# Fetching an expert block's output rows whole instead of in two halves

## The reference

```python
g_sel = jnp.argmax(g_logits, axis=-1)                       # one of 4 groups
top_p, top_i = lax.top_k(jax.nn.softmax(e_logits), 2)       # 2 of its 8 experts
# every (token, expert) pair gets a row; rows are sorted by expert, and each
# expert's rows are padded to blocks of 128
hid = jax.nn.silu(xb @ w_gate[e]) * (xb @ w_up[e])          # per block of 128 rows
y_rows = hid @ w_down[e]
y = zeros.at[row_token].add(y_rows * row_weight)            # two rows end on each token
```

## Time and profile before

| | |
|---|---|
| median of 3 runs | 1632.38 us (1631.96 to 1632.64) |
| profiled execution | 1631.91 us, its span 1630.2 us |
| busy, share of the span | PE 96%, DVE 78%, ACT 44%, POOL 37% |
| weights' queue (issued by SyncE), packets' time | 46.7% of the 16 DMA engines' span |
| GpSimd's queue, packets' time | 4.3% |
| output rows: fetches, scatters | 64 and 64 transfers |

### The profile page before, as it was taken

One profiled execution on the slowest core, in us unless ns is written; L12 is line 12 of the kernel. 1 busy time (PEld: TensorE's weight loads), 2 busy tenths in 40 slices (PEclk: granted clock), 3 DMA queues, 4 the chain that ended last, 5 costly groups with the idle time before them and its releaser, 6 DMA issues. The chain is left out here.

```text
span 1630.2 us, 26227 instructions
## 1 busy us (share of the span) xinstructions
PE 1572.4 (96%) x7516; PEld 1273.8 (78%) x7516; DVE 1268.1 (78%) x2301; ACT 716.7 (44%) x1219; POOL 601.5 (37%) x746
## 2 busy tenths in 40 slices
PE   6999999999999999999999998999999999999996
PEld 5778888878888788888888887777777777777774
DVE  6668868868778678688687786988878888888884
ACT  5333232223332323332322442765566666666662
POOL 2222131131130221321311311375666666655554
PEclk9999999999999999999999986999999999999999
DMA  4121121221121221211212665999999999999992
GB/s 158 39 83 54 50 78 34 59 73 46 41 74 42 60 72 45 65 50 49 79 33 72 198 229 187 352 361 369 365 375 370 378 369 372 356 367 364 375 362 81
DMA packets 142996, 292.76 MB, mean 180 GB/s; under 512 B 21596, under 2 KB 72204, under 8 KB 142896
## 3 DMA queue, kind: packets, MB, share of 16 engines
q1 hardware_dynamic: 127904, 266.29, 46.7%
q0 software_dynamic: 14992, 25.22, 4.3%
HBM read 291.81 MB, written 25.30 MB: 195 GB/s over the span
## 5 line engine op out<-in xcount | busy, mean ns | idle before, releaser
L2038 DVE TENSOR_TENSOR gu_lo<-w_gu,gu_hi 128x1024 fp32r<-128x1024 f32 x256 | 307.0, 1223 | 55.2 <-ACT gu_hi L1878 40.2
L1305 PE MATMUL proj<-uTh,wl 128*128 128x512 f32 x768 | 308.7, 402 | 7.4 <-issue 4.6
L1307 PE MATMUL proj<-uTh,wh 128*128 128x512 f32 x768 | 301.1, 392 | 0.0
L1306 PE MATMUL proj<-uTl,wh 128*128 128x512 f32 x768 | 300.0, 391 | 0.0
L1878 ACT ACTIVATE gu_hi<-w_gu 128x1024 fp32r<-128x1024 f32 x256 | 264.0, 1055 | 81.0 <-PE g_ps L1951 37.0
L556 POOL TENSOR_TENSOR wl<-raw,wh 128x512 fp32r<-128x512 f32 x96 | 129.5, 1366 | 382.3 <-ACT wh L643 382.3
L1305 PEld LDWEIGHTS proj<-uTh,wl 128*128 128x128 f32 x768 | 144.9, 189 | 37.9 <-issue 7.5
L1307 PEld LDWEIGHTS proj<-uTh,wh 128*128 128x128 f32 x768 | 144.7, 188 | 31.7
L696 ACT ACTIVATE xbc<-v 128x512 f32<-128x512 f32 x64 | 40.5, 633 | 292.1 <-DVE v L1021 292.1
L1306 PEld LDWEIGHTS proj<-uTl,wh 128*128 128x128 f32 x768 | 145.2, 189 | 28.6
L1021 DVE SCALAR_TENSOR_TENSOR v<-xr,cw,v 128x512 f32<-128x512 f32 x192 | 146.1, 761 | 14.7 <-DVE v L1017 0.5
(11 more groups left out here) (301 smaller groups left out, 3295.0 us busy)
## 6 DMA issues: line engine op xcount, KB each, us to landing
w_gu<-in_moe_w_gate_dram SPq DMA_DIRECT2D x128, 512.0 KB
w_gu<-in_moe_w_up_dram SPq DMA_DIRECT2D x128, 512.0 KB
w_d<-in_moe_w_down_dram SPq DMA_DIRECT2D x128, 512.0 KB
raw<-in_ssd_w_in_dram SPq DMA_DIRECT2D x96, 256.0 KB, 3.3
E<-acum_dram SPq DMA_DIRECT2D x64, 256.0 KB, 3.5
raw<-in_ssd_w_out_dram SPq DMA_DIRECT2D x28, 256.0 KB, 2.9
hacc<-in_x_dram SPq DMA_DIRECT2D x8, 512.0 KB, 7.5
out_dram<-hacc SPq DMA_DIRECT2D x8, 512.0 KB, 5.6
```

Source lines behind the costliest of these rows:

```text
L1305: nc.tensor.matmul(out, al, bh, start=start, stop=False)
L1306: nc.tensor.matmul(out, ah, bl, start=False, stop=False)
L1307: return nc.tensor.matmul(out, ah, bh, start=False, stop=stop)
L2038: vec.tensor_tensor(wl[:, j % RING, :], weights.gate_up(b, j), wh[:, j % RING, :].bitcast(F32), ALU.subtract).then_inc(w_lo, 1)
```

## The change

A fetch becomes one indirect transfer of 1024 columns per row, from `out` itself, with the token numbers in `stmp` as indices. Before it is issued it waits for both halves of the scatter. There is one semaphore per buffer instead of two, and `y_out` waits for it once, before the first half's add. Scatters stay in halves.

```diff
-        fetched = [[sem(f"fetched{b}{h}") for h in range(2)] for b in range(2)]
+        fetched = [sem(f"fetched{b}") for b in range(2)]
...
-                wait(pool, held_done, p, b, 4, -behind)
+                wait(pool, held_done, p, b, 3, -behind)
...
-            def fetch(p, b, h):
-
-                if b == 1:
-                    wait(pool, scattered[0][h], p, 0, 8, 16)
-                else:
-                    wait(pool, scattered[1][h], p, 0, 8, 0)
-                g.tensor_tensor(held[:, 1 + h, :], zero[:], zero[:], ALU.add).then_inc(held_done, 1)
-                g.indirect_dma_start(yb[:, b, h * 512:(h + 1) * 512], None, half_rows,
-                                     bass.IndirectOffsetOnAxis(sidx[:, b, h:h + 1].bitcast(U32), 0),
-                                     bounds_check=last_half, oob_is_err=False).then_inc(fetched[b][h], 16)
+            def fetch(p, b):
+
+                for h in range(2):
+                    if b == 1:
+                        wait(pool, scattered[0][h], p, 0, 8, 16)
+                    else:
+                        wait(pool, scattered[1][h], p, 0, 8, 0)
+                g.tensor_tensor(held[:, 1, :], zero[:], zero[:], ALU.add).then_inc(held_done, 1)
+                g.indirect_dma_start(yb[:, b, :], None, out,
+                                     bass.IndirectOffsetOnAxis(stmp[:, b, 0:1].bitcast(U32), 0),
+                                     bounds_check=last_token, oob_is_err=False).then_inc(fetched[b], 16)
...
-                    for h in range(2):
-                        fetch(p, b, h)
+                    fetch(p, b)
...
                 for j in range(2):
-                    wait(dve, fetched[b][j], p, 0, 8, 16)
+                    if j == 0:
+                        wait(dve, fetched[b], p, 0, 8, 16)
                     wait(dve, y_mm, p, b, 2, j + 1)
```

More of the change, by code:

```diff
@@ L1854, in _ @@
             last = pairs(pool, table_first)
-            wait(pool, held_done, last, 1, 4, 2)
+            wait(pool, held_done, last, 1, 3, 1)
             for h in range(2):
```

## The result

| | before | after |
|---|---|---|
| median of 4 runs each, us | 1632.51 | 1656.22 |
| lowest to highest | 1631.96 to 1635.44 | 1651.20 to 1671.47 |
| profiled execution, us | 1631.91 | 1657.26 |
| its span, us | 1630.2 | 1654.1 |

A forecast was written before the change was run, and what follows sets the result against it. The prediction took TensorE as the bound in the middle and latency at the end; 3.4 (end) + 1.2 (first blocks) + 0 (middle) = +4.6 us gave 1636.5 profiled, 1637.0 us as median, range 1634.0 to 1645.0.

The forecast's parts named there:

- The end: Last two blocks, nothing covering them: two whole fetches of 4.2 us each count fully, +3.4 us (+1.6 to +5.4).
- The first blocks: First expert blocks: whole fetches land later and TensorE waits for the adds, +1.2 us (-0.9 to +2.5).
- The middle: Expert blocks under streaming weights: the whole fetch lands before the next add is due, cost 0, 0.9 us left.
- The place: Middle: the whole fetch issues in the second half's place, 1294.34, leaving 8.5 us to the add at 1302.86.
- The landing: Middle, weights streaming: a whole fetch lands 7.6 us after its issue, bounds 6.4 and 8.8.
- the middle stalls: Rival, chance 0.18: with a landing of 8.8 the middle's loop outlasts 18.47 us, 0.3 per block, +7.5, 1644.5 us.
- The estimate from the page: Every whole fetch: the second half's 0.13 MB at 436 GB/s adds 0.3 us, sum about 1635; not used in forecast.
- The rival that went by 0.3: Rival, chance 0.20: second half costs 0.3 us, end +2.2, first blocks about +0.5, 1635.1 us, within the noise.

The follow-up runs named there:

- e12: Kernel before, half fetches each behind its own scatter, but the first add waits for both halves' fetches; 1635.69 us, ratio 1.0016.
- e13: Kernel before, but the first half's fetch waits for both halves of the scatter, adds wait for their own half; 1652.24 us, ratio 1.0102.
- e9: Changed kernel, but the last pair of blocks fetches in halves with a wait for each, as before; 1657.10 us, ratio 1.0138.
- e1: Changed kernel run once more, unchanged, against the kernel before on the same chip; 1661.16 us, ratio 1.0181.
- e4: Changed kernel with the gather of input rows issued ahead of the fetch instead of behind it; 1647.69 us, ratio 1.0096.
- e2: Kernel before, fetches in halves, but the first fetch waits for both scatters and the first add for both fetches; 1691.05 us, ratio 1.0345.
- e7: Kernel before with half of the weights' bytes loaded from block 2 on; 1629.97 us, ratio 0.9961.
- e3: Changed kernel, but its one fetch brings only the first 512 columns, the second half unread; 1632.58 us, ratio 1.0001.
- e14: Changed kernel fetching only one half of the columns, with the gather issued ahead of the fetch; 1634.63 us, one execution.
- e8: Changed kernel with half of the weights' bytes loaded from block 2 on; 1630.93 us, ratio 0.9967 to the kernel before.
- e11: Changed kernel, but VectorE begins a block's splits only once GpSimd has issued the fetch; 1655.69 us, ratio 1.0151.
- e10: Kernel before, halves everywhere, with the gather issued ahead of the two fetches; 1638.88 us, ratio 1.0039.
- e5: Changed kernel, with VectorE computing three unused tiles, both operands in SBUF, before its last adds; 1661.79 us, one execution.
- e6: Changed kernel, with VectorE computing four unused tiles, one operand in PSUM, before its last adds; 1657.50 us, one execution.

## Why the prediction was wrong

**The end: right up to the last scatter's issue, with nothing put behind it.** Forecast +3.4, measured +3.1. A whole fetch with quiet engines takes 4.33 and 4.36 us (4.2 forecast), 1.05 over the half's 3.30. The 0.53 us of issue ahead of the last fetch were not in the sum; the fetch of block 30 went out 0.7 us earlier after block 29's adds than before (1625.14 to 1631.73, against 1601.53 to 1608.82). These two errors cancel in part. e12 shows that the join at the adds alone makes this price (23.9), e13 that the join at the fetch alone makes 1.9 of it (22.7), and e9 takes it away.

Behind that issue the sum had no term, as if the rest stayed as it was. It is 2.9 us shorter to the end of the span. So of the +3.1 only +0.3 is left there (28.7 and 29.0; 29.1 in e1, 29.9 in e4), and the price of the end is far below the forecast. The cause is open.

**The first blocks: one landing too small.** The first whole fetch is added 20.6 us after block 0's adds, 20.9 forecast. The second is issued 31.2 us after them (31.3 forecast), in GpSimd's timeline after:

```profile
1073.73 2.03 POOL L1804 DMA_INDIRECT yb<-out_dram,stmp  x1
...
1092.76 1.70 POOL L1804 DMA_INDIRECT yb<-out_dram,stmp  x1 [0.52 <-issue]
```

but it is added 10.5 us later (1103.24), where I had 8.8. The first four blocks lose 3.9 us in place of 1.2.

**The middle: the step that failed.** It brings 15.6 of the 19.5 us from block 0 to 29. It read: "The whole fetch has the second half's place: issue at 1294.34, first add due at 1302.86, 8.5 us, against a landing of 7.6. So it costs **0**." Two terms of it were too good.
- The place. The fetch goes out 10.5 us after the adds, not 9.95, and 8.0 us are left, not 8.5. The 9.95 were those of one block; the median of the kernel before from 1150 to 1550 is 10.2. Now 0.53 us of issue stand ahead of the fetch in 29 of 31 blocks, where before 0.15 stood ahead of the first half in 25 of 31, and 0.15 ahead of the second. What brings them is open: e2 and e13 have them too, e12 mostly not, but e7 mostly does. And the scatters in front of it land in 6.9 in the median, not 6.4.
- The landing. It is 8.6, not 7.6. The base was wrong: I took 6.4, the scatters' median, for a half fetch in this place, and e3 measures 7.6. The 0.9 for the second half came out (1.0 by e3), but with luck: it was taken from quiet engines, and 0.6 of the 1.0 go when the gather behind the fetch does (e4 against e14: 0.4). The prediction said of that gather only that it isn't moved, and gave it no price.

The terms were off by 0.5 and 1.0 us in a sum with 0.9 us to spare. The rival "the middle stalls" had the mechanism, the loop and its three parts, and even the landing's upper bound, 8.8. It was too small because it kept 9.95: 0.3 us a block. The period is now 563.5 / 29 = 19.4 us against 544.0 / 29 = 18.8, 0.7 us more, 29 times.

**The estimate from the page.** The Trainium skill (DMA: Bandwidth & Descriptors, Anatomy of one DMA, SWDGE path) gave, by its fit, an estimate of 0.3 us for the second half of the rows. The runs show about 1 us, both quiet (4.35 against 3.30) and under the weights (8.6 against 7.6); only with the gather ahead is it near the estimate (0.4, one profile each). The rival that went by 0.3, with 1635.1 us, falls.

**What is shown and what isn't.** Shown: the loss in the middle needs the weights' traffic (e8) and the second half's bytes (e3), it comes with the join at the fetch and not with that at the adds (e13 against e12), and most of it needs the gather behind the fetch (e4). That VectorE's work makes the whole fetch late in the middle is not borne out (e11, and an issue of 1.05); of the second half in e2 and e13 it does hold that its issue is 1 us longer beside that work. Open: why a lone half takes 7.6 in this place when in e12, behind another half, the view gives 6.2 over both. The gather behind explains 0.2 of it at most (e14). The loads that SyncE issues at about the same time may do the rest; no run moved them. Open too is why the gather costs the whole fetch more than the half. No version beats the kernel before: those near or below its time leave work out (e3, e7, e8, e14) or keep the halves (e10, e12).

## What to carry to other kernels

Where a chain of transfers runs in a loop beside the compute (here add, scatter, fetch, add), write its period as a sum and compare it with the compute's period before merging two transfers in it: a merge joins their waits, and the chain then runs at the later of the two. Take each transfer's landing from one in the same place and under the same load, not from another kind, and spend the slack only if it exceeds the sum of what the terms may be off. The price at an uncovered end can be worked out to a few tenths of a microsecond from quiet rows as far as the last transfer's issue, but check what follows it as well: here 2.9 of 3.1 us came back behind it. The price under load can't be had from quiet rows. And look at what is issued behind a transfer, not only at what it waits for.

## What was not expected of the hardware

- Two half fetches that are released together are slower than one whole: the second issue took 2.06 us in e2 and 2.07 in e13, beside VectorE's splits, against 1.02 for the second half in its old place, in a gap of VectorE's.
- A whole fetch landed in 4.2 us on quiet engines (4.33 and 4.36 to the add) and in 8.6 in the median at 364 GB/s. A scatter of half rows took 3.4 at 212 GB/s and 6.9 at 364.
- GpSimd's issue of the same fetch took 1.66 us in place of 1.05 with VectorE working on operands in SBUF (e5), and 1.04 with one operand in PSUM (e6).
- With 32 to 34 fetches in place of 64, the span ends 5.0 to 5.3 us behind the last scatter's issue in place of 7.8 to 7.9.
- Up to block 0's adds, executions differ by up to 4.5 us whatever the kernel (1057.5 to 1062.0). It limits what a comparison of two single profiles shows.
- Whole fetches hardly save packets. GpSimd's queue on the two pages, before and after:

```profile
q0 software_dynamic: 14992, 25.22, 4.3%
q0 software_dynamic: 14480, 25.21, 4.1%
```

  Both fit 144 packets for a transfer of whole rows and 80 for one of half rows: two halves are 160.
